# Two FFN entries reordered: VectorE adds all squared tiles of the norm, TensorE makes one set of column sums

## What is computed

```python
xs = xs + ms[2] * os_
hs = rmsnorm(xs, g_ffn_norm[i]) * (1 + ms[4]) + ms[3]
xs = xs + ms[5] * swiglu(hs, w_ffn_gate[i], w_ffn_up[i], w_ffn_down[i])

def rmsnorm(x, g):
    y = x32 * lax.rsqrt(jnp.mean(x32 * x32, axis=-1, keepdims=True) + EPS)

def swiglu(h, wg, wu, wd):
    return (jax.nn.silu(h @ wg) * (h @ wu)) @ wd
```

## Time and profile before

| | us |
|---|---|
| median of 3 runs (1667.73 to 1671.55) | 1668.7 |
| the profiled execution | 1674.09 |
| its span, first to last instruction | 1672.3 |
| busy: TensorE / VectorE / ScalarE / GpSimd | 1621.5 / 1173.8 / 845.3 / 97.4 |
| mean granted TensorE clock | 0.986 |

### The profile page before, as it was taken

How to read it: one execution, slowest core, us unless ns; L and a number is a source line. 1 busy time by engine, 2 the same in 40 slices (tenths; PEclk the granted TensorE clock), 3 DMA queues, 4 the chain that set the end, 5 groups by cost and what they waited for, 6 DMA issues and landing times.

```text
span 1672.3 us, 28352 instructions
## 1 busy us (share of the span) xinstructions
PE 1621.5 (97%) x10988; PEld 1521.8 (91%) x10988; DVE 1173.8 (70%) x2033; ACT 845.3 (51%) x1460; POOL 97.4 (6%) x147
## 2 busy tenths in 40 slices
PE   6999999998999999999999999998989999999997
PEld 4878788798999999999989999998889999999997
DVE  5546465688857758767767787787898588586775
ACT  4634525366424525334547777786664254252443
POOL 1211110200000000000000000000000000000000
PEclk9999999999999999999999999999989999999998
DMA  9544453532433423332322222213122232232312
GB/s 320 165 158 139 126 191 113 190 94 74 122 108 102 120 75 87 121 92 92 99 69 79 64 76 64 69 55 120 56 76 70 83 96 72 74 89 64 102 40 87
DMA packets 230393, 171.06 MB, mean 102 GB/s; under 512 B 10643, under 2 KB 210998, under 8 KB 230262
## 3 DMA queue, kind: packets, MB, share of 16 engines
q1 hardware_dynamic: 216182, 120.37, 25.0%
q0 software_dynamic: 14080, 48.90, 8.6%
HBM read 160.32 MB, written 4.72 MB: 99 GB/s over the span
## 4 chain that ended last, share of the span: by engine, by line
PE 92%; DVE 4%; ACT 1%; issue 1%; DMA 1%; SPq 0%; POOL 0%; DVEq 0%; ACTq 0%; POOLq 0%
PE acc L833 45%; PE acc L1215 26%; PE side L1215 4%; PE side L1394 2%; PE side L1439 1%; PE acc L1439 1%; PE side L868 1%; PE work L1368 1%; DVE x L2663 1%; PE work L868 1%; PE side L1055 1%; PE acc L1037 0%; PE acc L868 0%; PE side L1037 0%; PE acc L1089 0%
## 5 line engine op out<-in xcount | busy, mean ns | idle before, releaser
L833 PE MATMUL acc<-h_hi,w_hi 128*128 128x320 f32 x1006 | 244.0, 324 | 6.5 <-DVE x L2663 2.0
L833 PE MATMUL acc<-h_lo,w_hi 128*128 128x320 f32 x1006 | 232.1, 312 | 0.0
L833 PE MATMUL acc<-h_hi,w_lo 128*128 128x320 f32 x1006 | 230.9, 311 | 0.0
L833 PEld LDWEIGHTS acc<-h_hi,w_hi 128*128 128x128 f32 x1006 | 166.4, 191 | 33.3 <-issue 23.1
L2663 DVE SCALAR_TENSOR_TENSOR x<-acc,mods,x 128x320 f32<-128x320 f32 (+2 forms) x249 | 94.1, 433 | 130.5 <-PE acc L833 130.3
L833 PEld LDWEIGHTS acc<-h_lo,w_hi 128*128 128x128 f32 x1006 | 171.1, 191 | 0.0
L833 PEld LDWEIGHTS acc<-h_hi,w_lo 128*128 128x128 f32 x1006 | 170.9, 191 | 0.0
L1215 PE MATMUL acc<-ax_hi,ff_hi 128*128 128x322 f32 x528 | 166.8, 316 | 0.8 <-issue 0.7
L1215 PE MATMUL acc<-h_hi,w_hi 128*128 128x322 f32 x616 | 167.3, 313 | 0.0
L1215 PE MATMUL acc<-ax_hi,ff_lo 128*128 128x322 f32 x528 | 165.1, 313 | 0.0
L1215 PE MATMUL acc<-ax_lo,ff_hi 128*128 128x322 f32 x528 | 165.1, 313 | 0.0
(11 more groups left out here) (461 smaller groups left out, 3622.6 us busy)
## 6 DMA issues: line engine op xcount, KB each, us to landing
a_raw<-in_w_ada_dram POOLq DMA_DIRECT2D x80, 512.0 KB, 6.2
ff_raw<-in_w_ffn_gate_dram SPq DMA_DIRECT2D x88, 256.0 KB, 3.4
ff_raw<-in_w_ffn_up_dram SPq DMA_DIRECT2D x88, 256.0 KB, 4.4
w_raw<-in_w_gla_in_dram SPq DMA_DIRECT2D x24, 512.0 KB, 3.8
ff_raw<-in_w_ffn_down_dram SPq DMA_DIRECT2D x32, 384.0 KB, 3.4
w_raw<-in_w_diff_qkv_dram SPq DMA_DIRECT2D x24, 512.0 KB, 4.0
ff_raw<-in_w_ffn_down_dram SPq DMA_DIRECT2D x32, 320.0 KB, 3.2
a_left<-in_w_ada_dram SPq DMA_DIRECT2D x8, 512.0 KB, 9.6
```

The lines of the kernel that those rows point to most:

```text
L833: mm = pe.matmul(out[:, s, 0:HALF + s * more], w[:, k * P:(k + 1) * P], a(k)[:, s * HALF:(s + 1) * HALF + s * more], start=(k == 0 and n = ...
```

## The change

Both FFN entries are rearranged. In `sum_squares`, `added_before` and `add_squares` the norms n = 1 and 3 are no longer special: VectorE adds tiles 6 and 7 as well (two more adds in `last_operands`, behind the split of P5's weights and behind the last operand), and TensorE makes one set of sums, of `sq_acc`, after the last quarters of P6 and P2. On ScalarE `ffn_begin` converts the weights of P4 and P3 and loads the Ln table before it keeps P6, has Ln behind the conversions of P7(1) and P6(1), and ends with a dummy Silu that loads Silu's table. On VectorE `ffn_begin` splits P3's weights and makes T13, T2 and P7(1)'s split before the variance, puts P6(1)'s split before `c22(0)`, and `c22_scaled(0)` and `gate_scaled(0)` right behind `c12_scaled(0)`. In `ffn_period` of tile 1 `c12_scaled(1)` comes behind P5(2)'s split, where it was the first operation of period 2. In layer 1's projection `late(0,2)` comes ahead of the split of unit 8, ScalarE's squares of tiles 0 to 2 go behind the scaled tile 5, and VectorE's first add behind the operands of tile 3.

```diff
@@ -327,7 +327,7 @@
-            return sum(KD - 3 if m in (1, 3) else KD - 1 if m in LATE else KD - 2 for m in range(1, n))
+            return sum(KD - 1 if m in LATE else KD - 2 for m in range(1, n))
@@ -908,7 +908,7 @@
-                parts = (sq_acc, sq[0], sq[1]) if n in (1, 3) else (sq_acc,) if n in LATE else (sq_acc, sq[(KD - 1) % 2])
+                parts = (sq_acc,) if n in LATE else (sq_acc, sq[(KD - 1) % 2])
                 for part, squares in enumerate(parts):
@@ -1257,10 +1257,9 @@
                         product(layer, 0, "P2", 0, JT - 1)
-                        sum_squares(n, 0, 2)
                         product(layer, 0, "P6", JT - 1)
                         product(layer, 0, "P2", JT - 1)
-                        sum_squares(n, 2, 3)
+                        sum_squares(n)
                         product(layer, 0, "P5")
@@ -1941,20 +1940,21 @@
-                kept(layer, 0, "P6")
                 weight_hi(layer, 0, "P4")
...
                 act.activation(small[:, 56:57], ones[:, 0:1], ACT.Ln)
+                kept(layer, 0, "P6")
+                weight_hi(layer, 1, "P7")
+                weight_hi(layer, 1, "P6")
                 act.wait_ge(var_ready, n)
                 act.activation(rstd[:, 0:T], var[:, :], ACT.Ln).then_inc(ln_ready, 1)
-                weight_hi(layer, 1, "P7")
-                weight_hi(layer, 1, "P6")
                 kept(layer, 1, "P1")
...
                 kept(layer, 1, "P6")
+                act.activation(small[:, 56:57], ones[:, 0:1], ACT.Silu)
@@ -2247,7 +2247,6 @@
                 operand_hi(1, "a11", 0)
-                square(0)
                 scaled_x(3, 1, x_updated(1))
@@ -2255,16 +2254,17 @@
                 split_hi(*out_unit(9), OUT_KT[9])
-                square(1)
                 scaled_x(3, 3, x_updated(3))
...
                 operand_hi(1, "s3", 2)
-                square(2)
                 scaled_x(3, 4, x_updated(4))
                 operand_hi(1, "s3", 3)
+                scaled_x(3, 5, x_updated(5))
+                square(0)
+                square(1)
+                square(2)
+                operand_hi(1, "s2", 0)
                 square(3)
-                scaled_x(3, 5, x_updated(5))
-                operand_hi(1, "s2", 0)
                 square(4)
@@ -2289,7 +2289,7 @@
             def add_squares(n, k):
-                if k == 0 or (k == KD - 1 and n not in LATE) or (k >= KD - 2 and n in (1, 3)):
+                if k == 0 or (k == KD - 1 and n not in LATE):
                     return
@@ -2759,7 +2759,7 @@
-            def last_operands(layer, add_six, add_seven):
+            def last_operands(layer, n, add_six, add_seven):
@@ -2777,9 +2777,11 @@
                 weight_lo(layer, 0, "P5")
+                add_squares(n, 6)
                 operand_lo(layer, "s2", 3)
...
                 operand_lo(layer, "h2", 3)
+                add_squares(n, 7)
@@ -2824,7 +2826,7 @@
                     add_squares(n, 5)
-                last_operands(0, sixth, lambda: add(7))
+                last_operands(0, n, sixth, lambda: add(7))
@@ -2883,26 +2885,26 @@
                 weight_lo(layer, 0, "P4")
+                weight_lo(layer, 0, "P3")
+                weight_sum(layer, 1, "T13")
+                weight_sum(layer, 1, "T2")
+                weight_lo(layer, 1, "P7")
                 variance(n, var[:, :])
-                weight_sum(layer, 1, "T13")
                 c11(layer, 0)
+                weight_lo(layer, 1, "P6")
                 c22(layer, 0)
-                weight_lo(layer, 0, "P3")
-                weight_sum(layer, 1, "T2")
-                c21(layer, 0)
-                weight_lo(layer, 1, "P7")
-                weight_lo(layer, 1, "P6")
                 weight_lo(layer, 1, "P2")
                 weight_lo(layer, 1, "P5")
+                c21(layer, 0)
                 weight_sum(layer, 1, "T4")
...
                 c12_scaled(layer, 0)
+                c22_scaled(layer, 0)
+                gate_scaled(layer, 0)
                 weight_lo(layer, 2, "P1")
...
                 weight_lo(layer, 2, "P7")
-                c22_scaled(layer, 0)
-                gate_scaled(layer, 0)
                 weight_lo(layer, 1, "P4")
@@ -2914,7 +2916,7 @@
                 if i > a:
-                    if i > 1:
+                    if i > 2:
                         c12_scaled(layer, i - 1)
@@ -2930,6 +2932,8 @@
                     weight_lo(layer, i + 1, "P5")
+                if i == 1:
+                    c12_scaled(layer, 1)
                 if i + 2 < b:
@@ -3274,9 +3278,9 @@
                 late(0, 1)
+                late(0, 2)
                 split_lo(*out_unit(8))
                 late(1, 0)
-                late(0, 2)
                 operand_sums(1, 0)
@@ -3286,15 +3290,15 @@
                 operands(1, 2)
+                operands(1, 3)
                 add_squares(3, 1)
-                operands(1, 3)
                 add_squares(3, 2)
...
                 add_squares(3, 4)
-                last_operands(1, lambda: add_to_x(*out_unit(9), KD - 1, 8), lambda: add_squares(3, 5))
+                last_operands(1, 3, lambda: add_to_x(*out_unit(9), KD - 1, 8), lambda: add_squares(3, 5))
             out_projection()
```

## The result

The changed kernel takes 1677.69 us in the median of 5 runs (1677.17 to 1679.45), the kernel before 1668.7 (1667.73 to 1671.55, five runs beside it): ratio 1.0049, 95% interval [1.0037, 1.0061]. The forecast was 1671.0 with a range up to 1674.5; the median lies above it. The profiled run of the changed kernel took 1677.8 us, its own median; that of before took 1674.09, 5.4 above its median. Trace against trace the change costs 3.7 us (span 1675.7 for 1672.3, so 3.4 within it), where 2.3 were forecast.

A forecast was written before the change was run, and what follows sets the result against it. TensorE was busy 97% of the span, but VectorE's queue was taken to set the FFN entries. Layer 0 0.1 us slower and layer 1 2.2, together 2.3, took the median from 1668.7 to 1671.0; range 1665.3 to 1674.5.

The forecast's parts named there:

- the last line of the sum: Whole run: both layers' 2.3 us added to the profiled run (1674.1 to 1676.4) and the median (1668.7 to 1671.0).
- it fell after 2.03 us: Out-projection of layer 1: granted clock was 0.50 after TensorE's 2.03 us wait, so longer waits were taken to lower it too.
- waits of 3.4 us in front of P3(1): Both FFN entries: TensorE's waits there stay at about 3.6 us and the clock falls in both layers.
- Rival 3: Both entries: the clock stays up in both shortened waits, -0.3 us, so 1668.4; chance 0.15.
- queue walk: FFN entries: each engine's queue followed in program order with trace spacings; `c22(0)` of layer 1 comes 4.0 us late.
- new wait for `u_t`: P5(2) in the entries: TensorE newly waits about 2 us for ScalarE.
- Layer 0: Its FFN entry: 0.1 us slower, bounds 1.35 faster and 1.3 slower.
- Layer 1: Its FFN entry: 2.2 us slower, bounds 1.1 and 4.4.
- waits of 1.9, 3.0 and 1.0 us: Layer 1's entry: new TensorE waits before P6(0), before its last quarter and before the sum, in that order.
- Rival 4: Both entries: new waits bring more falls of the clock, giving 1673.3 to 1674.4 us; chance 0.23.
- The ceiling: Column sums on TensorE: two sets less per entry save 2.14 us each, 4.3 us in all, at most.
- Rival 2: Both entries: TensorE's 4.3 us saving is kept, plus 1.0 in layer 0: 1663.4, at the least 1665; chance 0.12.

The follow-up runs named there:

- e14: The kernel before, unaltered, run once more for a trace of an early run: 1670.25 us, granted clock 0.991.
- e6: The kernel before with 24 matmuls that nobody reads added ahead of P3(1) in each FFN entry: median 1667.27 us, before 1672.92.
- e7: The changed kernel with 20 matmuls that nobody reads added ahead of P3(1) in each FFN entry: median 1674.97 us, before 1672.92.
- e5: The changed kernel run again, unaltered: median 1676.18 us, before 1672.92 on the same chip, ratio 1.0027.
- e8: The kernel before with one set of column sums in layer 0 alone and `late(0,2)` one step earlier: median 1666.87 us, before 1672.92.
- e2: The kernel before with one set of column sums and the two VectorE additions in both layers, nothing reordered: median 1671.86 us, before 1670.84.
- e9: e8 with 24 matmuls that nobody reads added ahead of P3(1) in both layers: median 1665.56 us, before 1670.9.

## Why the prediction failed

**The step that failed is the last line of the sum**, "the profiled run of 1674.1 becomes 1676.4, the median of 1668.7 becomes 1671.0". It says first that the trace is a sample of the runs behind the median, and second that the change costs the same in all of them. Neither holds. The trace came from a late run, 5.4 us above the median. What makes runs of before early is a clock that stays up behind TensorE's waits and in the attention (e14, e6). The changed kernel hardly ever has that gain: none of its 15 runs is early, and with the wait in front of P3(1) filled it gets 1.2 us (e7); by e7's trace other engines end last in its entries, and its new waits let the clock fall elsewhere. At low clock the change costs 2.6 us (e5), at high clock some 5.5 to 6 (the two runs of e7 at 0.993; the two of e5 at 0.990 and 0.991). The warning was there before the result: the profiled run lay 5.4 us above the median where the three runs spread over 3.8, and that should have raised the question where the trace had been slow.

**The clock**, the same step seen closer: "it fell after 2.03 us" was taken as a rule. It fell behind that wait in five of six traces of before, and not in e14. That the waits of 3.4 us in front of P3(1) let it fall was right in both layers. Rival 3 reckoned -0.3 us for a clock that stays up, over the base of a late run; over a base whose clock stays up too the filled waits leave a loss (e7 over e6, 7.7 us).

**The mechanism was right.** The queue walk held: `c22(0)` of layer 0 at 393.60 (forecast 393.8), of layer 1 at 1227.82 (1227.6); the sum at 1222.46 (not before 1222.2); x of tile 7 0.76 late (0.65); the wait for x 0.90 (1.0); `c12_scaled(1)` waits 3.07 and 3.14 (2.9 at half clock); TensorE's new wait for `u_t` 2.06 (about 2); the waits in front of P3(1) 3.40 and 3.41 (3.6). P5 of layer 0 came 1.2 us early (1.4), and the wait for the sum there was 0.47 (0.7). P3(0) of layer 0 waited 0.99 us for `c22(0)` (1.3) and came 0.4 early (0.3); in layer 1 P5(0) came 2.7 late (2.3) and P3(0) 3.6 late (3.4).

**Sizes that were off.** Layer 0: 0.5 us late for 0.1, within its bounds, and in e5's trace 0.5 early. Layer 1: 3.1 for 2.2 within bounds of 1.1 to 4.4. There the walk had waits of 1.9, 3.0 and 1.0 us ahead of and within P6(0) and the sum; measured were 2.48, 0.78 and 0.77. The clock fell behind the first, and P6(0) and P1(1) ran at its low level (0.50 from 1212 to 1218), in time that would otherwise have been waited: e7, where it was low only until 1214, waited 2.5 at the last quarter. Rival 4 named a low clock in this entry (1673.3 to 1674.4), but had it decide only for P5(0) to P3(0). In the changed kernel's trace it was low ahead of them, in e7's on P5(0). Over a late base rival 4's price of 4.6 to 5.7 us is too high for the 3.7 measured.

**The ceiling.** 4.3 us for two sets per entry: layer 0's 2.15 are real (e8), layer 1's are worth nothing (e2). Rival 2 was right about layer 0 alone, and the diff gave that away by the orders that it moved: without them (e8) layer 0 is 2.15 us early, with them 0.5 late to 0.5 early.

The prediction's shares for faster, unchanged and slower (0.12, 0.59, 0.29) should read 0.12, 0.60 and 0.28 by its own chances.

**What stays open:** why the clock falls behind one and the same wait in some runs; what sets the 0.9 us of spread in the attention of layer 1; and how much of the changed kernel's loss at high clock is queue and how much falls of the clock.

## What to carry to other kernels

Before a change is added to a median, set the profiled run's time and granted clock beside the other runs': where they differ, reckon the change once at either clock, because here the bound passed from TensorE to other engines, and the early runs went with it. Work that leaves TensorE is worth its time only where the engine that takes it has a hole at that place, read layer by layer. And a wait in the middle of a TensorE-bound kernel can cost more than its length; filling two of them with work that nobody needs gained 5.7 us here, where the ceiling of the change was 4.3.

## What the runs showed of the hardware that was not expected

One program, on one core of three chips, spreads over 7 us (1667.4 to 1674.5, 93 runs) with its granted clock, 0.986 to 0.993, while its waits for x and `up_n` differ by no more than 0.1 us over six traces. Behind one wait of 2.03 us the granted clock was at 2.4 GHz in one trace of this kernel and fell to 1.2 in five; in e2's trace, with the same wait, it stayed up. With 24 matmuls of 0.31 us each in front of it, a wait that had lasted 4.5 us was followed by full clock in both layers, in e6 and in e9.
